# A part's first seven-product tile: the third sum's low part and the combinations placed first on VectorE

## The reference, cut to what matters

```python
def _swiglu(h, wg, wu, wd):
    return (jax.nn.silu(h @ wg) * (h @ wu)) @ wd

x = x + 0.5 * mod[:, :, 2] * _swiglu(pre(x, 0), P['ffn_wg'][l, 0], P['ffn_wu'][l, 0], P['ffn_wd'][l, 0])
```

## Time and profile before

| what | value |
|---|---|
| median of 3 runs | 2518.48 us (2517.38 to 2518.59) |
| the profiled execution's own time | 2517.25 us |
| its span, first to last instruction | 2514.8 us |
| mean granted clock of TensorE | 0.999 of full |
| VectorE, ScalarE, GpSimd busy | 65%, 42%, 40% of the span |

### The profile page before, as it was taken

The page is one execution under the profiler, slowest core; times in us unless marked ns, Lnnn a source line. Parts: engine busy times, 40 slices in busy tenths (PEclk is TensorE's granted clock), DMA queues, the critical chain, the costliest instruction groups (busy, mean ns, idle before and its releaser), DMA issues. The chain is left out here.

```text
span 2514.8 us, 59172 instructions
## 1 busy us (share of the span) xinstructions
PE 2465.9 (98%) x23812; PEld 2338.1 (93%) x23812; DVE 1640.3 (65%) x3406; ACT 1046.4 (42%) x1986; POOL 1008.7 (40%) x768
## 2 busy tenths in 40 slices
PE   6999999999999999999999999999999999999999
PEld 4999998999988999999999999989998899899999
DVE  5677683377884466858666858635778824859493
ACT  3434343333465343434443434443344643435252
POOL 3443445333313444444444444443342235344443
PEclk9999999999999999999999999999999999999999
DMA  7353526322213424423532433552232135122232
GB/s 273 122 181 119 174 101 217 145 69 93 98 60 109 167 96 135 163 98 109 188 116 89 179 118 135 185 216 69 69 104 69 60 118 185 68 94 100 94 108 93
DMA packets 112645, 313.56 MB, mean 125 GB/s; under 512 B 19132, under 2 KB 45802, under 8 KB 95226
## 3 DMA queue, kind: packets, MB, share of 16 engines
q1 hardware_dynamic: 103424, 290.60, 33.5%
q10 hardware_dynamic: 8970, 19.44, 2.1%
HBM read 299.56 MB, written 10.66 MB: 123 GB/s over the span
## 5 line engine op out<-in xcount | busy, mean ns | idle before, releaser
L1090 POOL TENSOR_TENSOR w_lo<-raw,w_hi 128x512 fp32r<-128x512 f32 (+1 forms) x440 | 551.1, 1278 | 904.3 <-ACT w_hi L1221 875.8
L1097 POOL TENSOR_TENSOR w_lo<-raw,w_hi 128x512 fp32r<-128x512 f32 x228 | 331.0, 1466 | 447.0 <-ACT w_hi L1258 447.0
L2706 PE MATMUL bank<-h_hi,w_hi 128*128 128x260 f32 (+1 forms) x1312 | 380.7, 290 | 4.1 <-POOL w_lo L1109 3.5
L1221 ACT CAST w_hi<-raw 128x1024 fp32r<-128x1024 f32 (+2 forms) x164 | 216.5, 1320 | 384.9 <-PE bank L2708 271.6
L2707 PE MATMUL bank<-h_hi,w_lo 128*128 128x260 f32 (+1 forms) x1312 | 369.6, 282 | 0.0
L2708 PE MATMUL bank<-h_lo,w_hi 128*128 128x260 f32 (+1 forms) x1312 | 369.3, 281 | 0.0
L2853 PE MATMUL bank<-t_hi,w_hi 128*128 128x260 f32 x1216 | 345.7, 284 | 7.5 <-DVE u L2156 4.5
L2707 PE MATMUL bank<-mid_hi,w_lo 128*128 128x260 f32 x1232 | 348.6, 283 | 0.0
L2706 PE MATMUL bank<-mid_hi,w_hi 128*128 128x260 f32 x1232 | 348.6, 283 | 0.0
L2708 PE MATMUL bank<-mid_lo,w_hi 128*128 128x260 f32 x1232 | 347.3, 282 | 0.0
L2855 PE MATMUL bank<-t_hi,w_lo 128*128 128x260 f32 x1216 | 343.9, 283 | 0.0
(11 more groups left out here) (398 smaller groups left out, 6241.9 us busy)
## 6 DMA issues: line engine op xcount, KB each, us to landing
raw<-in_w SPq DMA_DIRECT2D x120, 1024.0 KB, 4.9
raw<-in_w SPq DMA_DIRECT2D x128, 512.0 KB, 4.1
ada_ring<-in_ada SPq DMA_DIRECT2D x68, 256.0 KB, 5.5
ada_ring<-in_ada SPq DMA_DIRECT2D x48, 320.0 KB, 5.3
raw<-in_w SPq DMA_DIRECT2D x32, 384.0 KB, 3.2
ada_ring<-in_ada SPq DMA_DIRECT2D x48, 192.0 KB, 5.2
ada_low<-in_ada SPq DMA_DIRECT2D x20, 256.0 KB, 4.8
out_y<-x ACTq DMA_DIRECT2D x4, 1040.0 KB, 13.9
```

The costliest lines, as they stand in the source:

```text
L1090: last = pool.tensor_tensor(w_lo[j][:, cols], raw[j][:, cols], w_hi[j][:, cols].bitcast(F32), ALU.subtract)
L1097: pool.tensor_tensor(place(w_lo, l, stage, slot, piece), src, place(w_hi, l, stage, slot, piece).bitcast(F32), ALU.subtract).then_inc(sema ...
L1221: s.copy(w_hi[j][:, 0:n], raw[j][:, 0:n]).then_inc(head_split[j], 1)
L2706: mm(out, wh(wb), xh(xb), start=(n == 0), stop=False)
```

## The change

For the first tile of parts 1 and 2 (`opens_part`): VectorE makes the low part of SUM_3 before that of SUM_1, ScalarE casts in the same order, and TensorE's SUM_3 product waits for two low parts in place of three, while the SUM_1 product now waits for the third. VectorE's `u2` and `u3` of that tile come ahead of the next tile's `sum1` and `sum2`. At the start of an FFN, ScalarE casts the gate half of tile 2 in tile 0, ahead of the second t cast, and no longer in tile 1. The idle matmuls ahead of the second and the fourth FFN are gone.

```diff
--- before.py
+++ after.py
@@ -260,7 +260,7 @@
 
 
 ADA_GAPS = {1: range(48, 64), 2: range(64, 74), 3: range(88, 104), 4: range(120, 136), 5: range(136, 144)}
-BUSY = {0: 17, 2: 8, 5: 3}
+BUSY = {0: 17}
 ADA_LOW, ADA_HIGH, ADA_SPARE = 4, 3, 4
 ADA_RING = 5
 
@@ -784,6 +784,10 @@
 
             return KIND.get((l, stage, slot))
 
+        def opens_part(key):
+
+            return EARLY[key][0] == ROW_11
+
         def early(key, piece):
 
             return 3 * SUMS_BEFORE[key] + 1 + EARLY[key].index(piece)
@@ -1290,7 +1294,7 @@
                         head(l, stage, r + 1, j, first + per * (2 * r + j + 1))
                 if stage[:2] == "do" and stage != f"down0{LAST}" and stage != f"down1{LAST}":
                     up = f"up{stage[4]}{int(stage[5]) + 1}"
-                    for piece in (SUM_2, ROW_11, SUM_1, SUM_3, ROW_22, ROW_12, SUM_4):
+                    for piece in (SUM_2, ROW_11, SUM_3, SUM_1, ROW_22, ROW_12, SUM_4):
                         cast(l, up, 0, piece)
 
             def last_stage(l, stage, sub, first, per):
@@ -1380,12 +1384,12 @@
                         t_head(l, f, 0)
                         high(0)
                         high(1)
+                        cast(l, stage, 2, SUM_1)
                         t_head(l, f, 1)
                     elif start and slot == 1:
                         silu(0)
                         silu(1)
                         t_head(l, f, 2)
-                        cast(l, stage, 2, SUM_1)
                         high(0)
                         cast(l, stage, 2, SUM_4)
                         high(1)
@@ -2022,8 +2026,9 @@
                     dve.wait_ge(piece_split, LOWS_BEFORE[key] + 1)
                     v.tensor_tensor(u0, u1, sum2[:], ALU.subtract).then_inc(sum_made, 1)
                 else:
-                    piece, src, cast_ = {"low2": (SUM_2, sum2[:], 1), "low1": (SUM_1, sum1[:], 3),
-                                         "low3": (SUM_3, g0, 4), "low4": (SUM_4, u0, None)}[step]
+                    third = opens_part(key)
+                    piece, src, cast_ = {"low2": (SUM_2, sum2[:], 1), "low1": (SUM_1, sum1[:], 4 if third else 3),
+                                         "low3": (SUM_3, g0, 3 if third else 4), "low4": (SUM_4, u0, None)}[step]
                     if cast_ is None:
                         dve.wait_ge(head_split[j], slot_use(l, stage, slot // 2) + 1)
                     else:
@@ -2146,14 +2151,18 @@
                         lead("low4")
                         low(1)
                     else:
-                        lead("sum1")
-                        lead("sum2")
+                        if not opens_part(key):
+                            lead("sum1")
+                            lead("sum2")
                         dve.wait_ge(early_full, early(key, SUM_2))
                         dve.wait_ge(p1_copied, before + 1)
                         v.tensor_tensor(u2[:], gate_bank(1), p1[:], ALU.add).then_inc(combined, 1)
                         dve.wait_ge(early_full, early(key, SUM_3))
                         dve.wait_ge(combined, 5 * before + 1)
                         v.tensor_tensor(u3[:], gate_bank(0), u2[:], ALU.add).then_inc(combined, 1)
+                        if opens_part(key):
+                            lead("sum1")
+                            lead("sum2")
                         lead("low2")
                         wait_main(dve, main_unit(l, stage, 4 * slot))
                         dve.wait_ge(combined, 5 * before + 2)
@@ -2187,7 +2196,7 @@
                         for step in ("sum1", "sum2", "low2", "sum3"):
                             sums(l, up, 0, step)
                     if up is not None and n == KT - 2:
-                        for step in ("low1", "low3"):
+                        for step in ("low3", "low1"):
                             sums(l, up, 0, step)
                     if up is not None and n == KT - 1:
                         for step in ("sum4", "low4"):
@@ -2873,7 +2882,7 @@
 
                 def sum3_product():
                     pe.wait_ge(t_ready, t0 + 2)
-                    pe.wait_ge(sum_split, 4 * before + 3)
+                    pe.wait_ge(sum_split, 4 * before + (2 if opens_part(key) else 3))
                     take_main(1, use)
                     piece_product(gate_bank(0), SUM_3, t_hi[:, 1], t_lo[:, 1], True, True).then_inc(early_full, 1)
 
@@ -2886,6 +2895,7 @@
                     row11_product()
                     sum3_product()
                 take_main(2, use)
+                pe.wait_ge(sum_split, 4 * before + 3)
                 piece_product(up_bank(1), SUM_1, t_hi[:, 0], t_lo[:, 0], True, True).then_inc(main_full, 1)
                 pe.wait_ge(t_ready, t0 + 4)
                 pe.wait_ge(piece_split, lows + 2)
```

## The result

The changed kernel took 2534.64 us (median of 3 runs, 2531.53 to 2537.93) against 2518.48: ratio 1.0062, 95% interval [1.0048, 1.0076]. It is slower, as forecast, but by 16.2 us where 9.9 were forecast, and 2.6 us above the range. Three first readings: the page's busy times, TensorE's list of waits, and the timelines of the two tiles.

What follows compares the result with a forecast made beforehand. TensorE is 98% busy, but VectorE's list up to low(0) sets the second tile's start. 3.3 + 7.2 - 0.6 = +9.9 us on 2517.25 gives 2527.2; with 1.2 for the median, 2528.4, range 2521 to 2532.

Steps and rivals of the forecast that it cites:

- VectorE's list is the bound: Parts 1 and 2: VectorE works without a gap, so the second tile's ROW_11 waits for low(0); u2 to low(0) becomes 9.17 us.
- A tile: First seven-product tile after a down stage of six weight blocks per slot; four tiles, +0.83 us each, +3.3 in all.
- B tile: First seven-product tile after a down stage of eight weight blocks per slot; four tiles, +1.80 us each, +7.2 in all.
- The uncovered cast, 0.83: VectorE before the second tile's low2: nothing covers ScalarE's cast of the second sum any more, costing 0.83 us.
- Low3 before low1, 0: First tile: SUM_3's 1.5 us wait goes without saving time; taken as 0, between -1.07 and +1.07 per A tile.
- Gate cast, -0.6 and three times 0: Part 0, third tile: moving the cast gains 0.6 us in the first FFN and 0 in the other three.
- Loads, 0: SP issues slot 3's load up to 1.8 us later; first read a tile later, 10.0 us, so no cost.
- Idle matmuls, 0 if the clock stays: Second and fourth FFN starts: without the eight and three, TensorE waits longer, to the same moment; 0.
- the clock falls: Rival, chance 0.08: at two part starts without idle matmuls, half-speed stretches of 3.4 us lose 3.4 us together: 2531.8.
- some 2 us in all eight parts: Sign: new TensorE waits on line 2853, released by line 2113, of some 2 us in all eight parts.
- Faster (the collisions go): Rival, chance 0.10: VectorE's instructions slip past all GpSimd collisions; -7.8 us, 2510.7.
- no change (they go in part): Rival, chance 0.12: collisions avoided in part, or part 0's gate waits come back as gains; about 2521.

Runs made afterwards that it cites:

- e8: Changed kernel with low2 of the next tile moved behind the combination that follows it, covering ScalarE's cast of the second sum: 2535.28 us, ratio 1.0068.
- e3: Kernel before with only the gate cast of part 0's third tile moved ahead of the second t cast: 2518.02 us, ratio 0.9999.
- e4: Kernel before with only the idle matmuls ahead of the second and fourth FFN removed: 2518.69 us, ratio 0.9996.
- e1: Kernel before with only u2 and u3 moved ahead of the next tile's sum1 and sum2: 2533.26 us, ratio 1.0056.
- e2: Kernel before with only the third sum's cast and low part put first, SUM_3 waiting for two low parts: 2523.86 us, ratio 1.002.
- e10: Changed kernel with the eight and three idle matmuls ahead of the second and fourth FFN put back: 2539.50 us, ratio 1.0081.
- e12: The changed kernel itself, measured again: 2531.63 us, ratio 1.0052.
- e11: Changed kernel with the FFN starts' idle matmuls put back and seven more ahead of ROW_11 of each part's second tile: 2526.94 us, ratio 1.0032.
- e6: e2 with 14 identity products added ahead of ROW_22 in each A tile: 2518.26 us, ratio 0.9996 against the kernel before.
- e9: Kernel before with VectorE's list of a part's first seven-product tile rewritten, one order for A and one for B: 2514.22 us, ratio 0.9982.

## Why the prediction was right, and where it was wrong

**VectorE's list is the bound** (right). From `u2` to `low(0)`: forecast 9.17 us, measured 9.16 and 9.18. The list is not VectorE's work alone, as the prediction read it: ScalarE's cast and GpSimd's low part stand in it (e8). The second ROW_11: forecast +0.83 in each A tile and +1.80 in each B tile, measured +0.92, +0.78, +0.86, +0.77 and +2.09, +1.80, +1.78, +1.81, in all 10.8 us where 10.5 stood in the sum (9.8 if the first part of e3 or e4 is the start). e1 shows that the moved sums alone do it.

**The uncovered cast, 0.83** (right as a time, not as a cause). The gap of 0.74 is there, but e8 closes half of it and wins nothing, since GpSimd's low part of ROW_11 is behind the same casts and `sum3` ends behind it. What the list lost beside the 1.33 us of the two sums is the 0.87 that `u2` and `u3` take ahead of `sum2`; that the uncovered cast, priced at 0.83, came to the same size is luck.

**Low3 before low1, 0** (right inside the change, wrong by itself). The collision went from the second low part to `sum4`, 1.76 to 1.74, as worked out. With the sums left where they were (e2) the exchange costs 5.6 us, in the tiles through the clock; in the changed kernel `u2` comes earlier and the wait before ROW_22 is 1.16 or less (it is left in three A tiles, where two were forecast), and no stretch stands behind it.

**Gate cast, -0.6 and three times 0** (right). e3 shows no difference, and the wait at the up product, 1.80 for 1.55. Between e1 and the changed kernel, which start their first FFN equally late (3.8 us), part 1 begins 0.4 to 0.7 us earlier with the cast moved (+0.56 and +0.91 against before, +1.29 in e1). Of the two profiles without a slow stretch at the start-up, before and e10, the one with the cast moved begins it 0.73 earlier; 0.6 was forecast.

**Loads, 0** (nothing in the list of waits speaks against it; not tried by itself).

**Idle matmuls, 0 if the clock stays** (right in time, for another reason). The clock does not stay: at one or both FFN starts it falls. It costs nothing (e4), because part 0 waits behind it anyway.

**The step that failed** is the price of a wait. The sum counts the 2 us at each second tile as 2 us, and the rival "the clock falls" stood at two part starts only, with 3.4 us and a chance of 0.08. The starts were the harmless place (e4: no difference). The eight new waits, which the prediction itself had listed as "some 2 us in all eight parts", were never held against the earlier trace rows, and it is there that the clock falls: 1.5 us for each such tile, three in one profile, none in another, five in e1. That the present 1.46 us of the earlier trace rows did no harm was taken as evidence for waits of 2 us; it was none.

In the profiled execution (2537.93, its span 21.3 above before's, where the sum had 9.9) the account is 10.8 for the first tiles, 4.8 for the second tiles, 4.8 between part 2 of one FFN and the first seven-product tile of the next, across the two mixers, and 0.9 before part 1 of the first FFN. So the second tiles are under half of what the forecast lacks here. In the profile of e12, whose span is 15.0 above before's, they are 0.2, and the mixers 3.5. For the mixers the sum had no term; they hold stretches at 0.5 too (549, 617 and 1863 in the first profile, 549 and 1860 in the second, 1848 in the kernel before), and what brings these is open. e11, with one there (613) and none behind a second tile, comes to 2526.94, 1.5 us from the forecast of 2528.4. The size of the miss is itself uncertain: the five executions of e12 have a median of 2531.63, 3.2 us above the forecast and just inside the range.

The Trainium skill, "TensorE: Matmul & The Clock Gate", Part 1, cited in the prediction for the idle matmuls, says that the slow clock is the default and activity lifts it; e6 agrees, at a place where the prediction did not look: with identity products in the wait the clock stays at 1.00 where it was 0.51.

Faster (the collisions go) and no change (they go in part) were wrong for the reason given against them: the casts that release the stretched instructions came in the same order. e9 shows that the gain supposed there exists, if the list itself is reordered.

**Left open.** Which of several equal waits is followed by a slow stretch was not settled; it changes between executions of one kernel. The 4.8 us around the mixers are measured and only in part explained. In all six profiles of kernels that leave waits of 2 us or more in their seven-product tiles (the changed kernel twice, e1, e2, e8, e10) the way across the two mixers, taken from and to the same tiles, is 1.7 to 9.3 us longer than in the kernel before; in the other seven it is between 2.7 shorter and equal. No run tests whether the one brings the other. A piece of them is there without the change, too: TensorE stands 1.8 to 1.9 us in the mixer, near 545 us, for nothing that the profile names (the row is from the changed kernel's list of waits):

```profile
PE bank L3140 <- issue: 1.9, 1, 1.9
```

This gap is in nine of the 14 profiles, that of before among them, and the stretch near 549 follows it in six of the nine and never stands without it. What the gap is, and where the stretches near 615 and 1863 come from, was not tried.

## What to carry to other kernels

Where a saturated TensorE shows no slack, ask of a removed wait which engine's list the work stands in: if the interval between two releases on that engine is equal in every case, TensorE's wait only moves. Then price a moved wait by its length in one piece, not by the sum: here two waits of 1.3 and 1.0 us cost what they are, one of 2.5 us cost 1.3 us more in three of four tiles, and some identity products in front of it (counted so that they end before the wait does) gave that back. And look for the gain in the list of the engine that is the bound, here by moving its stretched instructions out of another engine's way.

## What the runs showed of the hardware

A VectorE instruction with two inputs in SBUF that starts while GpSimd makes a low part ended some 0.55 us behind GpSimd's, whenever it started: `sum3` took 1.46 us in the changed kernel and 1.80 in e8 for 0.69 of work. One with an input in PSUM was not touched: line 2169 of the changed kernel took 0.43 us in the same tile, and in e9, where such instructions stand beside GpSimd's, `up1` and both products take 0.42 to 0.44. The Trainium skill, "SBUF — State Buffer", section "Who interferes with whom", says that a VectorE instruction with at most one SBUF input does not contend with GpSimd (outside what it calls the 2-port perf modes), and that one with two contends with a GpSimd instruction that reads SBUF; these rows agree.

A stretch at half clock can be free or not within the first tiles of one FFN: 3.4 us of it left a loss of 1.2 us at 950 in e10 and none at 921 in the changed kernel, 30 us earlier, since the next tiles had waits to give.
